# Issuing nine small transfers of each attention head from ScalarE's queue instead of SyncE's

## The reference

```python
def layer(x, conv_hist, attend, lp, lam, lam_init):
    z = rmsnorm(x, lp['g_pre_mix']) @ lp['w_in']
    u, va, q, k, vb = jnp.split(z, ...)                    # 8 heads of 128 each
    u = jax.nn.gelu(u)
    va = rmsnorm(jax.nn.gelu(va).reshape(B, T, H_A, HD_A), lp['g_v_a'])
    a_out = chunk_gmlp(u, va, lp['w_s'], lp['b_s'])         # u * (tril(w_s) @ va + b_s), chunks of 128
    o = attend(q, k, vb, lam)                               # softmax(q1 k1) - lam * softmax(q2 k2), times v
    b_out = (rmsnorm(o, lp['g_subln']) * (1.0 - lam_init)).reshape(B, T, W_B)
    mix = jnp.concatenate([a_out, b_out.astype(a_out.dtype)], axis=-1) @ lp['w_out']
    h = x + rmsnorm(mix, lp['g_post_mix'])
    up = rmsnorm(h, lp['g_pre_ffn']) @ lp['w_up']
    c, new_hist = causal_dwconv(conv_hist, up, lp['w_conv'], lp['b_conv'])
    gate, val = jnp.split(c, 2, axis=-1)
    y = (jax.nn.gelu(gate) * val) @ lp['w_down']
    return h + rmsnorm(y, lp['g_post_ffn']), k, vb, new_hist, va
```

## Time and profile before

| | |
|---|---|
| time, median of 3 runs | 2724.88 us (2723.86 to 2728.06) |
| profiled execution | 2726.88 us, span 2724.9 us |
| TensorE busy | 2536.7 us, 93% of the span |
| VectorE / ACT / GpSimd busy | 52% / 34% / 26% |
| DMA | 411.85 MB, mean 151 GB/s |
| chain that ended last | PE 81%, DVE 8%, DMA 4%, SPq 3% |
| key page, issue to landing | 5.7 us (median of 128) |
| `V` / `ws` / `qT`, issue to landing | 6.3 / 6.1 / 3.5 us (medians of 8) |

### The profile page before, as it was taken

How to read it: one execution, slowest core, us unless ns; L and a number is a source line. 1 busy time by engine, 2 the same in 40 slices (tenths; PEclk the granted TensorE clock), 3 DMA queues, 4 the chain that set the end, 5 groups by cost and what they waited for, 6 DMA issues and landing times.

```text
span 2724.9 us, 49317 instructions
## 1 busy us (share of the span) xinstructions
PE 2536.7 (93%) x19556; PEld 2420.0 (89%) x19556; DVE 1409.2 (52%) x1916; ACT 934.9 (34%) x1321; POOL 718.0 (26%) x544
## 2 busy tenths in 40 slices
PE   7999999999999992599999999999999899999994
PEld 7999976677769991599999999999999899999994
DVE  5000144444443227988888888888887302121115
ACT  5111143443333212444444444444444222221221
POOL 3333311221213335011111111111111433333333
PEclk9999999999999996799999999999999899999997
DMA  4333599999985212133333333333334332424221
GB/s 174 105 106 118 169 334 346 349 347 344 339 319 187 79 59 102 48 108 109 107 110 111 111 110 112 108 107 106 107 107 148 123 137 86 148 85 155 78 78 70
DMA packets 130809, 411.85 MB, mean 151 GB/s; under 512 B 16161, under 2 KB 28193, under 8 KB 128481
## 3 DMA queue, kind: packets, MB, share of 16 engines
q1 hardware_dynamic: 129088, 404.98, 43.0%
q0 software_dynamic: 1568, 4.72, 0.4%
HBM read 373.06 MB, written 36.33 MB: 150 GB/s over the span
## 4 chain that ended last, share of the span: by engine, by line
PE 81%; DVE 8%; DMA 4%; SPq 3%; issue 3%; ACT 1%; POOL 1%; DVEq 0%; ACTq 0%; POOLq 0%
PE pb L1833 11%; PE pb L1835 11%; PE pb L1834 11%; PE pb L381 7%; PE pb L385 7%; PE pb L383 7%; PE pb L1859 7%; PE pb L1864 7%; PE pb L1862 7%; DMA pg<-in_kpages 2%; PE pb L1691 2%; PE pb L1627 1%; SPq L488 1%; DVE mix L1333 1%; DVE ul L1341 1%
## 5 line engine op out<-in xcount | busy, mean ns | idle before, releaser
L1833 PE MATMUL pb<-reg,uh 128*128 128x288 f32 x2464 | 732.1, 297 | 33.1 <-DVE reg L1414 27.3
L1835 PE MATMUL pb<-reg,ul 128*128 128x288 f32 x2464 | 729.9, 296 | 0.0
L1834 PE MATMUL pb<-reg,uh 128*128 128x288 f32 x2464 | 726.3, 295 | 0.0
L1833 PEld LDWEIGHTS pb<-reg,uh 128*128 128x128 f32 x2464 | 465.1, 189 | 34.7 <-issue 33.4
L825 ACT ACTIVATE uh<-ua 128x1024 fp32r<-128x1024 f32 x308 | 325.2, 1057 | 453.1 <-PE pb L1835 208.8
L1834 PEld LDWEIGHTS pb<-reg,uh 128*128 128x128 f32 x2464 | 468.3, 190 | 0.0
L1835 PEld LDWEIGHTS pb<-reg,ul 128*128 128x128 f32 x2464 | 465.9, 189 | 0.0
L1341 DVE TENSOR_TENSOR ul<-ua,uh 128x1024 fp32r<-128x1024 f32 x308 | 375.4, 1219 | 110.1 <-ACT uh L825 110.0
L367 POOL TENSOR_TENSOR wl<-wraw,wh 128x1024 fp32r<-128x1024 f32 x108 | 260.3, 2411 | 629.4 <-ACT wh L362 629.4
L381 PE MATMUL pb<-xh,wh 128*128 128x288 f32 x1792 | 393.5, 301 | 24.5 <-DVE xl L1090 17.2
L385 PE MATMUL pb<-xh,wl 128*128 128x288 f32 x1792 | 385.9, 297 | 0.0
(11 more groups left out here) (226 smaller groups left out, 3146.1 us busy)
## 6 DMA issues: line engine op xcount, KB each, us to landing
ua<-in_wstream SPq DMA_DIRECT2D x264, 512.0 KB, 3.6
pg<-in_kpages SPq DMA_DIRECT2D x128, 512.0 KB, 5.7
pg<-in_vpages SPq DMA_DIRECT2D x128, 512.0 KB, 5.4
wraw<-in_wstream SPq DMA_DIRECT2D x112, 512.0 KB, 3.5
g_d<-gv SPq DMA_DIRECT2D x44, 288.0 KB, 2.1
xl<-g_d SPq DMA_DIRECT2D x8, 1152.0 KB, 10.3
xres<-in_xT SPq DMA_DIRECT2D x4, 1152.0 KB, 8.9
h_d<-mix SPq DMA_DIRECT2D x4, 1152.0 KB, 4.1
```

The lines of the kernel that those rows point to most:

```text
L1833: te.matmul(out, whk, xhk, start=opens and k == 0, stop=False, skip_group_check=again)
L1834: te.matmul(out, whk, xlk, start=False, stop=False, skip_group_check=again)
L1835: m = te.matmul(out, wlk, xhk, start=False, stop=k == HK - 1, skip_group_check=again)
```

## The change

The three groups of small transfers become functions with the issuing engine as an argument. For head 0 SyncE still issues all nine, before the first round. For heads 1 to 7 ACT issues them: `head_loads(j + 1)` behind the last `s_exp` of round j, `token_loads(j + 1)` (`ws`, `wb`, `V`, `vnew`) between the square root and the GELU at the end of round j, and `bias_load(j)` (`bsb`) behind the first `p_exp` of round j. `bsb` gets a semaphore of its own, and GpSimd's wait counts two transfers a round instead of three. ACT's last round is written out apart from the loop. SyncE keeps pages and weight units. Each transfer still waits for the last reader of its own tile, and its bytes stay as they are.

```diff
--- before.py
+++ after.py
@@ -304,8 +304,8 @@
 
     pg_landed = [sem(f"pages_landed{i}") for i in range(PSLOTS // 2)]
     pg_used = sem("pages_used")
-    hq_landed, sq_landed, hv_landed, sv_landed, g_landed = (sem(x) for x in (
-        "head_qk_landed", "sample_q_landed", "head_v_landed", "sample_v_landed", "gmlp_landed"))
+    hq_landed, sq_landed, hv_landed, sv_landed, g_landed, b_landed = (sem(x) for x in (
+        "head_qk_landed", "sample_q_landed", "head_v_landed", "sample_v_landed", "gmlp_landed", "bias_landed"))
     names_h = ("st_copied s_max pscore_ready pexp_done pneg_ready pw_done snew_ready snew_masked nmx_ready "
                "sexp sT_ready sT_copied wT_ready wT_copied u_evac ugelu va_evac vgelu vsq_ready vssq_ready "
                "vsd_done va_gained vaT_ready vtok_copied ws_masked spv_ready osb_ready oT_ready pv_ready "
@@ -424,6 +424,32 @@
     def by_seq(ap):
         return ap.rearrange("p (b n) -> p b n", b=DB)
 
+    def head_loads(eng, q, j):
+
+        wait_past(eng, s["pscore_ready"], 4 * j)
+        q.dma_start(qT[:], zq_d[bass.ds(j, 1), :, 0:SEQ].rearrange("a p n -> (a p) n")).then_inc(hq_landed, 16)
+        q.dma_start(kT[:], k_out[bass.ds(j, 1), :, 0:SEQ].rearrange("a p n -> (a p) n")).then_inc(hq_landed, 16)
+        wait_past(eng, s["snew_ready"], j)
+        q.dma_start(qb[:].rearrange("p h n -> p (h n)"),
+                    qs_d[:, bass.ds(j, 1), :].rearrange("p a n -> p (a n)")).then_inc(sq_landed, 16)
+        q.dma_start(knew[:].rearrange("p h n -> p (h n)"),
+                    ks_d[:, bass.ds(j, 1), :].rearrange("p a n -> p (a n)")).then_inc(sq_landed, 16)
+
+    def token_loads(eng, q, j):
+
+        wait_past(eng, s["gm_ready"], j)
+        q.dma_start(ws[:], wsT[bass.ds(j, 1)].rearrange("a p n -> (a p) n")).then_inc(g_landed, 16)
+        q.dma_start(wb[:], wblk[bass.ds(j, 1)].rearrange("a p n -> (a p) n")).then_inc(g_landed, 16)
+        wait_past(eng, s["pv_ready"], j)
+        q.dma_start(V[:], v_out[bass.ds(j, 1)].rearrange("a b p n -> p (a b) n")).then_inc(hv_landed, 16)
+        wait_past(eng, s["spv_ready"], j)
+        q.dma_start(vnew[:], vs_out[bass.ds(DT * j, DT)].rearrange("t h n -> t (h n)")).then_inc(sv_landed, 16)
+
+    def bias_load(eng, q, j):
+
+        wait_past(eng, s["ao_sample"], j)
+        q.dma_start(bsb[:], bs[bass.ds(j, 1), :].to_broadcast([P, P])).then_inc(b_landed, 16)
+
     block = nc.Block().__enter__()
 
 
@@ -471,17 +497,6 @@
                 sp.dma_start(vs_out[:, bass.ds(2 * i + t, 1), :].rearrange("p a n -> p (a n)"),
                              vt[t][0:NS, 4, :]).then_inc(v_stored[t], 16)
 
-        def head_loads(j):
-
-            wait_past(sp, s["pscore_ready"], 4 * j)
-            sp.dma_start(qT[:], zq_d[bass.ds(j, 1), :, 0:SEQ].rearrange("a p n -> (a p) n")).then_inc(hq_landed, 16)
-            sp.dma_start(kT[:], k_out[bass.ds(j, 1), :, 0:SEQ].rearrange("a p n -> (a p) n")).then_inc(hq_landed, 16)
-            wait_past(sp, s["snew_ready"], j)
-            sp.dma_start(qb[:].rearrange("p h n -> p (h n)"),
-                         qs_d[:, bass.ds(j, 1), :].rearrange("p a n -> p (a n)")).then_inc(sq_landed, 16)
-            sp.dma_start(knew[:].rearrange("p h n -> p (h n)"),
-                         ks_d[:, bass.ds(j, 1), :].rearrange("p a n -> p (a n)")).then_inc(sq_landed, 16)
-
         def page(n, j):
 
             slot = n % PSLOTS
@@ -499,25 +514,18 @@
         sp.wait_ge(s_stored, 32)
         sp.wait_ge(p_landed, 16)
         v_loads(2, first_page=0)
-        head_loads(0)
+        head_loads(sp, sy, 0)
         v_loads(3, first_page=4)
 
         sp.wait_ge(v_stored[0], 16 * H)
         sp.wait_ge(v_stored[1], 16 * H)
+        token_loads(sp, sy, 0)
+        bias_load(sp, sy, 0)
 
         def batch_loads(j, last=False):
             for n in range(8, 12):
                 page(n, j)
             w_load(U_HEADS, 0, 4, j)
-            wait_past(sp, s["gm_ready"], j)
-            wait_past(sp, s["ao_sample"], j)
-            sp.dma_start(ws[:], wsT[bass.ds(j, 1)].rearrange("a p n -> (a p) n")).then_inc(g_landed, 16)
-            sp.dma_start(wb[:], wblk[bass.ds(j, 1)].rearrange("a p n -> (a p) n")).then_inc(g_landed, 16)
-            sp.dma_start(bsb[:], bs[bass.ds(j, 1), :].to_broadcast([P, P])).then_inc(g_landed, 16)
-            wait_past(sp, s["pv_ready"], j)
-            sp.dma_start(V[:], v_out[bass.ds(j, 1)].rearrange("a b p n -> p (a b) n")).then_inc(hv_landed, 16)
-            wait_past(sp, s["spv_ready"], j)
-            sp.dma_start(vnew[:], vs_out[bass.ds(DT * j, DT)].rearrange("t h n -> t (h n)")).then_inc(sv_landed, 16)
             for n in range(12, 24):
                 page(n, j)
             for c in range(1, 3):
@@ -526,7 +534,6 @@
                     page(n, j)
             w_load(U_HEADS, 3, 4, j)
             if not last:
-                head_loads(j + 1)
                 for n in range(8):
                     page(n, j + 1)
 
@@ -705,7 +712,7 @@
             for c in range(4):
                 w_split_hi(U_V, c, 4, i)
 
-        def batch(j):
+        def batch(j, first=False, last=False):
             wait_past(act, s["spv_ready"], j)
 
             def copy_scores(g_):
@@ -733,6 +740,8 @@
             for g_ in range(3):
                 copy_scores(g_)
                 p_exp(g_)
+                if g_ == 0 and not first:
+                    bias_load(act, sc, j)
             w_split_hi(U_HEADS, 0, 4, j)
             copy_scores(3)
             act.wait_ge(s["nmx_ready"], j + 1)
@@ -742,6 +751,8 @@
             act.wait_ge(s["nmx_ready"], j + 1)
             for g_ in range(2, 5):
                 s_exp(g_)
+            if not last:
+                head_loads(act, sc, j + 1)
             w_split_hi(U_HEADS, 1, 4, j)
             act.wait_ge(s["va_evac"], j + 1)
             sc.activation(vg[:], vg[:], ACT.Gelu_apprx_tanh).then_inc(s["vgelu"], 1)
@@ -768,12 +779,15 @@
             w_split_hi(U_HEADS, 3, 4, j)
             act.wait_ge(s["sss_ready"], j + 1)
             sc.activation(osq[:], pb[:, 4, 0:NS], ACT.Sqrt, scale=1.0 / HD, bias=EPS).then_inc(s["ssd_done"], 1)
+            if not last:
+                token_loads(act, sc, j + 1)
             act.wait_ge(s["u_evac"], j + 1)
             sc.activation(ug[:], ug[:], ACT.Gelu_apprx_tanh).then_inc(s["ugelu"], 1)
 
-        batch(0)
-        with act.Fori(1, DB) as j:
+        batch(0, first=True)
+        with act.Fori(1, DB - 1) as j:
             batch(j)
+        batch(DB - 1, last=True)
 
 
         act.wait_ge(w_used, U_OUT)
@@ -992,7 +1006,7 @@
         pl.affine_select(out=maskd[:], in_=maskd[:], compare_op=ALU.is_ge, fill=NEG, base=0,
                          pattern=[[-1, P]], channel_multiplier=1).then_inc(ready, 1)
         with pool.Fori(0, DB) as j:
-            pool.wait_ge(g_landed, 48 * j + 48)
+            pool.wait_ge(g_landed, 32 * j + 32)
             w_split_lo(U_HEADS, 0, 4, j)
 
             pl.affine_select(out=ws[:], in_=ws[:], compare_op=ALU.is_ge, fill=0.0, base=0,
@@ -1245,7 +1259,7 @@
             v.tensor_scalar(osb[:], pb[:, 7, 0:2 * P], rs[:, 0:1], None, ALU.mult).then_inc(s["osb_ready"], 1)
 
             dve.wait_ge(s["gm_ready"], j + 1)
-            dve.wait_ge(g_landed, 48 * j + 48)
+            dve.wait_ge(b_landed, 16 * j + 16)
             wait_past(dve, s["a_stored"], 16 * j)
             v.tensor_tensor(ao[:, 0:SEQ].rearrange("p (b n) -> p b n", b=4),
                             pb[:, 2, :].rearrange("p (b n) -> p b n", b=4),
```

## The result

The changed kernel takes 2713.41 us (median of 6, 2711.59 to 2715.28) against 2725.65 us for the kernel before beside it (6 runs): ratio 0.9955, 95% interval 0.9942 to 0.9968, 12.2 us faster. The prediction was 2708 us with a range of 2695 to 2720. The profiled execution took 2715.28 us, its span is 2713.3 us.

What follows compares the result with a forecast made beforehand. TensorE, busy 93% of the span, bounds the kernel, waiting for late key pages in the attention rounds. Terms -24.0 - 5.2 + 10.5 + 2.0 = -16.7 us gave 2708 us, range 2695 to 2720.

Steps and rivals of the forecast that it cites:

- page waits, rounds 1 to 7: TensorE's waits for key pages at line 1627 would all go, as pages 0 and 12 are issued earlier: -24.0 us.
- clock drops: Matmuls behind the page waits run at a lowered clock; three of four such drops would go: -5.2 us.
- stall by ACT's token issues: Token issues before the round-end GELU delay ACT's exponentials and TensorE's second prompt scores: 1.5 us a round, +10.5 us.
- first round: Five token transfers now ahead of page 8 delay the third page group; with a possible clock drop: +2 us.
- rival 3: Only removing the head transfers counts, clock drops stay, the stall hides in remaining waits: 2716 us, chance 0.10.
- two readings of ACT's issues: Token issues at round end: in series with ACT's arithmetic, stall 2.0 us; sequencer running ahead, 0.9 us; 1.5 taken.
- Page 15 is there at 475 to 476 ... Both waits go, 24.0 us: Third round: page 15 lands before TensorE wants it at 477.94 or 477.1, so waits before pages 8-11 and 12-15 vanish.
- nine transfers at 1.28 us each: Pages 8 to 11, a weight unit and pages 12 to 15 take 11.5 us from about 462.5, plus 1 to 2 us.
- ACT's place (c): Four token transfers between square root and GELU, without cover: 2.5 us of issuing against 0.5 us of slack.
- Place (a): Four head transfers behind the last sample exponential, covered by ACT's later wait for TensorE: cost 0, uncovered up to 1.8 us.
- Rival 2: The line of transfers is the bound and pages land no earlier: 2726 us, no change, chance 0.13.

Runs made afterwards that it cites:

- tokens_only: Changed kernel with the head transfers back on SyncE ahead of page 0 and head 0's tokens in their old place; only token transfers on ACT: 2713.44 us, ratio 0.9957.
- heads_only: Changed kernel with the five token transfers back in SyncE's queue behind page 11 in all rounds; only the four head transfers on ACT: 2721.18 us, ratio 0.9988.
- dummy_issues: Kernel before plus four tiny loads into a scratch tile, issued by ACT ahead of the GELU of u each round: 2725.68 us against 2727.63, ratio 0.9992.
- late_stores: sp_all_late with GpSimd's stores of the two mixer outputs moved into the next round, behind its first weight split: 2699.45 us, ratio 0.9900.
- sp_all_late: Kernel before with all nine small transfers in SyncE's queue behind value page 31, GpSimd's masks later, nothing on ACT: 2704.69 us, ratio 0.9913.
- tokens_early: Changed kernel with ACT's four token transfers issued earlier, ahead of the last weight split where ACT idles: 2715.72 us, ratio 0.9967.

## Why the prediction was right, and where it wasn't

| step | forecast | measured |
|---|---|---|
| page waits, rounds 1 to 7 | -24.0 | -15.3 (24.0 to 8.7) |
| clock drops | -5.2 (three of four) | -6.1 (all four gone; TensorE's busy time 390.9 to 384.8) |
| stall by ACT's token issues | +10.5 | +6.5 (5.9 to 12.4) |
| first round | +2.0 | +4.6 |
| sum, in the profiles | -16.7 | -10.3; the spans differ by 11.6, of which 1.2 lie outside the rounds |

The direction and the stretch were right, and of the mechanism the main part: SyncE's issues ahead of page 12 were the cost, as tokens_only shows against heads_only. The number owes something to luck. In the profiles the waits were put 8.7 us too high and the first round 2.6 too low, but the stall 4.0 too high and the clock 0.9 too low, and these partly cancel. The time is even nearer to rival 3's 2716 us than to 2708. But of what that rival assumed only one thing was so, that the stall hides in waits (dummy_issues): the head transfers, which it let count, gave little, and the clock drops, which it kept, went.

Of the two readings of ACT's issues the overlapped one was right: 0.9 us a round forecast for it, 0.93 measured, and the first issue starts under the weight split. Taking 1.5, between the readings, was 4 us too much. The Trainium skill's queue of 8 on ScalarE (TensorE: Matmul & The Clock Gate, "Architectural detail: the array is 16× 32×32, not 1× 128×128") agrees with these rows, which don't show its depth.

The step that failed is "Page 15 is there at 475 to 476 ... Both waits go, 24.0 us": 16 to 17 us into the round. In the third round page 15 is issued 11.7 us into the round (469.68 and 4.14 for the four, less some 0.33 of its own, against a start of 461.82), 3.8 us earlier than before, as forecast. But it takes 8.1 us to land (473.49 to 481.58) where it took 5.3, and TensorE gets it 19.9 us into the round instead of 20.9: of 3.8 us of earlier issue about 1 arrived. The windows behind the first scores of that round:

```profile
463.82:471.82 8.00, 7.05 (x54) 4.93 (x53) 3.87 (x9) 5.03 (x9) 2.45 (x3) 1.00 0.95 297
471.82:481.82 10.00, 8.88 (x69) 6.54 (x71) 5.42 (x16) 2.98 (x10) 0.00 (x0) 1.00 1.02 410
```

The sum put nine transfers at 1.28 us each and let page 15 land when its bytes were through. Two things were missing in it. In the first 8 us the DMA engines moved 297 GB/s and not 408; that makes some 2.2 us, an estimate from these two rates. And a transfer lands later than its bytes take: of the weight units in the rounds of the kernel before, 512 KB each like a page, the quickest landed 3.4 us behind its issue, 2.1 above the 1.28 (an estimate too). Either could be most of the 3 to 4 us by which page 15 came late, and they may overlap: no run tries them apart, so this part of the cause stays open. The kernel before would have warned me: I read a DMA share of about 1 as a full line, and its trace has this window too, against 408 with pages alone:

```profile
451.00:455.00 4.00, 4.00 (x53) 2.47 (x53) 2.20 (x5) 0.85 (x7) 0.55 (x1) 1.00 0.96 253
```

The stores of the mixer outputs are a part of the slow stretch: late_stores (on sp_all_late; on the changed kernel it wasn't tried) takes 544 KB of them out of it, 1.4 us at 408 GB/s, and 7.3 us of waits before group 2 go, 1.0 us a round. That is no more than the 1 to 2 us that the sum had for them. A smaller slip is in the size of the four head transfers: by the list ahead of the prediction they are 672 KB, 1.7 us, and not 544 KB. And six of the slices in the earlier trace rows are at 9 tenths, the seventh is at 8.

The sum for ACT's place (c) was right as a stall and wrong as a loss. dummy_issues and tokens_early both fit this: a microsecond more or less ahead of the page waits doesn't reach the end while those waits are there. In the table the terms of waits and stall are therefore not independent: in tokens_early the stall is gone, the waits are 14.2 us, and the time is no better.

The first round was mis-sized by 2.6 us. I moved the group wait by the 3.1 us of issues; the row shows the group at 356.56 after 4.81 us of waiting instead of 1.35, 3.5 more. Most of the miss is the clock: TensorE is busy 2.7 us longer in this round (57.56 us against 54.89), where I had put 0.5 for a drop of 1.7 that might come.

Place (a), the head transfers, cost ACT nothing, as forecast: in the third round they are issued from 489.19 under the exponentials, and TensorE's sum of squares isn't waited for. That their going from ahead of page 0 would help was wrong: heads_only has the waits at 21.4 us. The likely reason is that pages 8 to 11 can't be issued before the first scores are done, however early pages 0 to 7 start.

Rival 2 (the transfers are the bound) held a part of the truth: page 15 lands only 1 us earlier. The Trainium skill's sentence (DMA: Bandwidth & Descriptors, "Issuing engines are not separate DMA queues"), that a second issuing engine saves issue time only, agrees with these runs: sp_all_late has all nine on SyncE and is faster. Its "usually small relative to the DMA itself" is true here of each transfer, 0.33 to 0.69 us of issue against 6.1 to landing for `ws`; but five in a row and ahead of a page that is waited for were 3.7 us a round and most of the gain.

## What to carry to other kernels

Before moving transfers to another engine's queue, look for a gap in the present one: the cost was five issues in front of a contested page, and a later place in the same queue did more than a second queue. A wait is a buffer: here a cost placed ahead of it was free (dummy_issues) and a saving ahead of it brought nothing (tokens_early), so take the waits off from the last one back. Judge a busy line of transfers by its GB/s against the best stretch, not by its share; where the rate is low, look for what else is in it, small transfers and the stores of other queues. And in a sum over such a line give the last transfer its time to land, not only its bytes.

## What the runs showed of the hardware

- ACT issues a transfer in 0.33 to 0.65 us (changed kernel, rounds 1 to 7; SyncE's small ones take 0.33 to 0.69 in the earlier trace rows) and does so while its arithmetic is still at work: 461.99 with the split of 461.69 to 462.75 running. What is delayed in these rows is the arithmetic behind the issues in the queue.
- Small transfers issued by ACT at the end of a round landed sooner than SyncE's behind pages: medians of 3.2 us for `V` and 2.4 for `ws`, against 6.3 and 6.1 before. Queue and place changed together, so which of them did it isn't shown; `qT`, issued by ACT among value pages, took 5.9 instead of 3.5.
- A transfer of 512 KB takes 1.28 us at 408 GB/s, but landed 3.4 to 7.9 us behind its issue (weight units in the rounds of the kernel before), and page 15 of the third round 5.3 us before and 8.1 in the changed kernel.
- 544 KB of stores from GpSimd's queue cost the pages issued around them 1.0 us a round in waits, at the turn of a round. 20 us later they cause no new wait of TensorE that shows, though value pages then take 6.2 us to land instead of 5.5 (medians).
- Waits of up to 2.5 us came without a clock drop in the changed kernel (2.47 us in its second round), and in the kernel before drops came behind waits of 1.94, 2.01, 2.04 and 3.42 us but not behind those of 1.96 and 2.40; the waits alone don't say when it falls.
